# A decoder layer in three-pass fp32: the low halves of the weights made by accumulating DMAs instead of GpSimd

## The reference, cut to what matters

```python
x = x + 0.5 * swiglu(rms_norm(x, g_ffn1), w1_ffn1, w3_ffn1, w2_ffn1)     # 1024 -> 2816 -> 1024
z = rms_norm(x, g_mix) @ w_in + b_in                                     # 1024 -> 1792: q, k, v, u, v_gate
# head group A: windowed attention with sinks; head group B: gated spatial mixing in chunks of 128
x = x + concat(A, B) @ w_out + b_out
x = x + 0.5 * swiglu(rms_norm(x, g_ffn2), w1_ffn2, w3_ffn2, w2_ffn2)
x = x + sigmoid(rms_norm(x, g_ple) @ w_ple_gate) * (p @ w_ple_proj)
y = rms_norm(x, g_final)
```

## Time and profile before

| | |
|---|---|
| median of 3 runs | 1050.07 us (1049.6 to 1050.35) |
| span of the profiled execution | 1047.1 us, the one time that the page gives of it |
| PE busy | 1023.1 us, 98% |
| POOL busy | 473.8 us, 45% |
| DVE busy | 467.2 us, 45% |
| ACT busy | 340.0 us, 32% |
| DMA | 94.98 MB, 91 GB/s on average |
| chain that ended last | PE 93%, DVE 4%, ACT 1%, issue 1%, DMA 1% |

### The profile page before, as it was taken

One profiled execution on the slowest core, in us unless ns is written; L12 is line 12 of the kernel. 1 busy time (PEld: TensorE's weight loads), 2 busy tenths in 40 slices (PEclk: granted clock), 3 DMA queues, 4 the chain that ended last, 5 costly groups with the idle time before them and its releaser, 6 DMA issues.

```text
span 1047.1 us, 20237 instructions
## 1 busy us (share of the span) xinstructions
PE 1023.1 (98%) x8397; PEld 1009.3 (96%) x8397; DVE 467.2 (45%) x631; ACT 340.0 (32%) x505; POOL 473.8 (45%) x221
## 2 busy tenths in 40 slices
PE   6999999999999999999999999999999999999996
PEld 5999999999999999999989999999999999999895
DVE  6644544454421212356776554444454421121675
ACT  5222232223222222564534232223222322222232
POOL 2443434444455554321438444444444455555451
PEclk9999999999999999999999999999999999999998
DMA  5333232323232236322123232323233233323202
GB/s 177 100 89 97 83 100 80 100 80 121 71 96 90 90 95 181 88 60 61 41 72 101 81 102 81 100 82 98 85 95 91 86 91 96 90 90 96 85 22 82
DMA packets 179861, 94.98 MB, mean 91 GB/s; under 512 B 12010, under 2 KB 177220, under 8 KB 179804
## 3 DMA queue, kind: packets, MB, share of 16 engines
q1 hardware_dynamic: 175792, 90.76, 29.6%
q10 hardware_dynamic: 4028, 3.63, 1.1%
HBM read 91.82 MB, written 3.59 MB: 91 GB/s over the span
## 4 chain that ended last, share of the span: by engine, by line
PE 93%; DVE 4%; ACT 1%; issue 1%; DMA 1%; SPq 0%; DVEq 0%; ACTq 0%
PE ps L1126 89%; PE ps L1163 1%; PE ps L1364 1%; DMA x_rows<-in_x_prompt_dram 1%; PE ps L1337 1%; DVE rs_t L777 0%; PE ps L1158 0%; DVE mix_lo L1015 0%; DVE rs_i L774 0%; PE ps L1152 0%; DVE xg_lo L811 0%; DVE p_lo L1080 0%; DVE g_rows L985 0%; ACT xg_hi L491 0%; PE ps L1385 0%
## 5 line engine op out<-in xcount | busy, mean ns | idle before, releaser
L677 POOL TENSOR_TENSOR w_lo<-w_raw,w_hi 128x1024 fp32r<-128x1024 f32 x168 | 410.0, 2441 | 525.4 <-ACT w_hi L421 525.4
L1126 PE MATMUL ps<-xg_hi,w_hi 128*128 128x260 f32 x1760 | 360.3, 286 | 0.0
L1126 PE MATMUL ps<-xg_hi,w_lo 128*128 128x260 f32 x1760 | 355.9, 284 | 0.0
L1126 PE MATMUL ps<-xg_lo,w_hi 128*128 128x260 f32 x1760 | 355.3, 284 | 0.0
L421 ACT ACTIVATE w_hi<-w_raw 128x1024 fp32r<-128x1024 f32 x168 | 178.0, 1059 | 422.5 <-PE ps L1126 422.4
L1126 PEld LDWEIGHTS ps<-xg_hi,w_hi 128*128 128x128 f32 x1760 | 272.5, 190 | 1.3 <-issue 0.8
L1126 PEld LDWEIGHTS ps<-xg_hi,w_lo 128*128 128x128 f32 x1760 | 272.8, 189 | 0.0
L1126 PEld LDWEIGHTS ps<-xg_lo,w_hi 128*128 128x128 f32 x1760 | 271.8, 189 | 0.0
L1126 PE MATMUL ps<-h_hi,w_hi 128*128 128x260 f32 x704 | 142.0, 283 | 0.0
L1126 PE MATMUL ps<-h_hi,w_lo 128*128 128x260 f32 x704 | 141.5, 282 | 0.0
L1126 PE MATMUL ps<-h_lo,w_hi 128*128 128x260 f32 x704 | 141.3, 282 | 0.0
(11 more groups left out here) (209 smaller groups left out, 684.7 us busy)
## 6 DMA issues: line engine op xcount, KB each, us to landing
w_raw<-in_w_ffn_dram SPq DMA_DIRECT2D x120, 512.0 KB, 3.8
w_raw<-in_w_ffn_dram SPq DMA_DIRECT2D x16, 384.0 KB, 3.1
w_raw<-in_w_in_dram SPq DMA_DIRECT2D x10, 512.0 KB, 3.8
w_raw<-in_w_ple_gate_dram SPq DMA_DIRECT2D x8, 512.0 KB, 3.6
x_rows<-in_x_prompt_dram SPq DMA_DIRECT2D x4, 512.0 KB, 5.2
w_raw<-in_w_in_dram SPq DMA_DIRECT2D x8, 256.0 KB, 3.6
w_raw<-in_w_out_dram SPq DMA_DIRECT2D x16, 128.0 KB, 2.9
w_raw<-in_w_out_dram SPq DMA_DIRECT2D x8, 256.0 KB, 3.1
```

Source lines behind the costliest of these rows:

```text
L677: nc.gpsimd.tensor_tensor(w_lo[:, n % RING, :], w_raw[:, n % RING, :], w_hi[:, n % RING, :].bitcast(F32), ALU.subtract).then_inc(w_lo_read ...
L1126: ins = pe.matmul(ps[:, 2 * p + h, 0:HALF], w[:, n % RING, k * P:(k + 1) * P], m_[:, sk, h * HALF:(h + 1) * HALF], start=(first and i == 0 ...
```

## The change

ACT writes the negated high half into `w_lo` beside the high half into `w_hi`. POOL no longer subtracts: it starts a DMA that adds `w_raw` onto `w_lo`, so that `w_lo` holds raw - high. Its completion counts 16 on one of three semaphores `lo_in`, one for each slot; SP's loads and PE's units wait for those in place of `w_lo_ready`. `w_hi_ready` now counts when both ACT instructions are done. POOL's loops over the FFN units are written out. Nothing else differs.

```diff
-        w_hi_ready, w_lo_ready = sem("w_hi_ready"), sem("w_lo_ready")
+        w_hi_ready = sem("w_hi_ready")
+        lo_in = [sem(f"lo_in{i}") for i in range(RING)]
...
             def load(n, step, it, src, width=KD * P):
 
                 if n >= RING:
-                    sp_.wait_ge(w_lo_ready, at(n - RING + 1, step, it))
+                    sp_.wait_ge(lo_in[n % RING], at(16 * (n // RING), 16 * step // RING, it))
...
                     act.wait_ge(unit_done, at(n - RING + 1, step, it))
-                nc.scalar.activation(w_hi[:, n % RING, :], w_raw[:, n % RING, :], ACT.Copy).then_inc(w_hi_ready, 1)
+                nc.scalar.activation(w_hi[:, n % RING, :], w_raw[:, n % RING, :], ACT.Copy)
+                nc.scalar.activation(w_lo[:, n % RING, :], w_raw[:, n % RING, :], ACT.Copy,
+                                     scale=-1.0).then_inc(w_hi_ready, 1)
...
                 pool.wait_ge(w_hi_ready, at(n + 1, step, it))
-                nc.gpsimd.tensor_tensor(w_lo[:, n % RING, :], w_raw[:, n % RING, :],
-                                        w_hi[:, n % RING, :].bitcast(F32), ALU.subtract).then_inc(w_lo_ready, 1)
+                pool.dma_start(w_lo[:, n % RING, :], w_raw[:, n % RING, :],
+                               accum_op=ALU.add).then_inc(lo_in[n % RING], 16)
...
             def ffn(up, down, stat):
-                split_lo(up + 3)
-                split_lo(up + 4)
-                with pool.Fori(0, (KF - 1) // 3) as it:
-                    for r in range(3):
-                        split_lo(up + 2 * (1 + r) + 3, 6, it)
-                        split_lo(up + 2 * (1 + r) + 4, 6, it)
+                for n in range(up + 3, up + 2 * KF + 3):
+                    split_lo(n)
                 clear_ssq(stat + 1)
-                with pool.Fori(0, KD // 2) as it:
-                    for m in range(2):
-                        for c in range(3):
-                            split_lo(down + 3 * m + 3 + c, 6, it)
-                        add_square(stat + 1, m, 2, it)
+                for m in range(KD):
+                    for c in range(3):
+                        split_lo(down + 3 * m + 3 + c)
+                    add_square(stat + 1, m)
...
-                pe.wait_ge(w_lo_ready, at(n + 1, step, it))
+                pe.wait_ge(lo_in[n % RING], at(16 * (n // RING + 1), 16 * step // RING, it))
```

More of the change, by code:

```diff
@@ L360, in _ @@
                     n, j = IN + u, int(name[1])
-                    sp_.wait_ge(w_lo_ready, n - RING + 1)
+                    sp_.wait_ge(lo_in[n % RING], 16 * (n // RING))
                     for c in range(NKV):
@@ L1252, in _ @@
                             pe.wait_ge(z_scaled, u - 1 if u > 3 else 1)
-                        pe.wait_ge(w_lo_ready, n + 1)
+                        pe.wait_ge(lo_in[n % RING], 16 * (n // RING + 1))
                     if u == 0:
```

## The result

The changed kernel takes 1053.75 us, the median of 11 runs (1052.92 to 1060.40); the kernel before, run beside it, takes 1049.77 (11 runs, 1047.70 to 1051.29). The medians lie 4.0 us apart. The ratio is 1.0057, with a 95% interval of 1.0038 to 1.0075: slower, by 4 to 8 us. The ratio weighs all runs, here and in the experiments, and is larger than that of the medians because five of the 11 runs lie above 1055. The profiled execution took 1053.27 us and spans 1051.5. The result lies inside the predicted range, but on the other side of no change from the forecast of 1048.0.

The account below looks back on a forecast made before the run. PE was taken to bound the kernel, busy 1023.1 of 1047.1 us. Span 1047.1 - 4.8 (gains) + 2.7 (losses) = 1045.0, plus 3.0 from span to median run, gave 1048.0 us; range 1044.5 to 1085.

Parts of the forecast that it names:

- IN+3, and all FFN units, fit: Low halves, 7.5 us from high-half start, arrive within the room (8.1 us at mixer unit IN+3): no loss.
- T: Time from POOL's issue of the accumulating DMA to its completion, taken as 5.4 us.
- unit 0: First weight unit: low half ready at 20.9 in place of 19.44, a loss of 1.5 us.
- bound by engine time: Load 1.8 us plus accumulation at most twice that: 5.4 of a unit's 5.77 us on the DMA engines, close to full.
- Unit 2: Early weight unit with two more ACT copies ahead of it: a loss of 0.2 us.
- OUT+3: Output projection unit: low half needs 7.5 us of 6.5 us room, a loss of 1.0 us.
- Mixer: Gains at the spatial step: 1.3 us of PE's wait and 1.2 us from the lower clock behind it.
- stat_out and p: PE's waits for the diagonal ahead of stat_out, 1.6 us, and for p's low half, 0.7 us, go.
- Ring too short: Rival, chance 0.29: the weight ring is too short for the DMA, slower; it decides from T = 6.4.
- Gains do not come: Rival, chance 0.13: POOL still holds VectorE or mixer waits only move; gains of 4.8 shrink to 2, 1050.5 to 1052 us.
- VectorE holds up the issue: Rival, chance 0.06: POOL waits for VectorE instructions when issuing, T grows by 2.1 to 7.5, 1053.5 us.
- The DMA is quick: Rival, chance 0.12: T at most 4.4, hardly any loss, 1045.3 to 1046 us.

Follow-up runs that it names:

- Copies_late: Changed kernel with the two cache copies taken from ACT's burst at the mixer's start and issued by SP about 80 us later: 1050.89 us, ratio 1.0019.
- pool_in3: Changed kernel with the low half of unit IN+3 alone made by GpSimd's subtraction, without ACT's negated copy for it: 1049.28 us, ratio 1.0004.
- plain_copy: Changed kernel with GpSimd's 168 DMAs copying w_raw into w_lo, the addition left out: 1048.97 us in one execution.
- pool_three_late: Changed kernel with low halves of units 0, IN+3 and OUT+3 subtracted by GpSimd, cache copies issued 80 us later by SP: 1050.11 us, ratio 0.9996.
- pool_three_defer: pool_three_late with ACT's negated copy of unit IN+13 also moved behind the turned probabilities of the last attention item: 1046.99 us, ratio 0.9977.
- act_copy_only: Kernel before with ACT's negated copy into w_lo added and GpSimd adding w_raw instead of subtracting, no DMA: 1053.30 us, ratio 1.0044.

## Why the prediction failed where it did

**The step that failed** is "IN+3, and all FFN units, fit", as far as it speaks of IN+3. It was costed at 0, and the place cost 8.9 us, more than the whole distance from the forecast to the result (1053.75 - 1048.0 = 5.75). Copies_late and pool_in3 show that it is this place: the one takes its wait from 5.62 to 2.29 us, the other takes it away, and with it 6.9 of the 8.9 us and the measured loss. The other 2.0 come with a wait for ACT, which the prediction had at nothing as well. The step had three holes. It took T as one number for all places, from a median; the same engines carry the cache copies there, and T was 9.4. It took the start of the high half from before (417.73), although ACT issues DMAs ahead of it and one of those issues grew from 1.46 to 4.53 us. And it priced the clock only as a gain. The range held because it reached to a T of 9.3; but the forecast behind that upper end, all units paying, is not what happened. That the result lies in it is luck.

**T itself** was well sized: 5.4 forecast, 5.7 measured, unit 0 at 4.7. From the start of a high half to POOL's issue it is 2.3 us (420.93 to 423.22), 2.1 forecast. The bound by engine time also held: 48.1 + 30.2% of the engines, and no FFN unit waits. The second operand was costed at 1.8 us on a base of 3.8; plain_copy shows 2.8 on a base of 2.9, so two errors cancelled, and the median was met by luck. On the rule quoted there (the Trainium skill, DMA: Bandwidth & Descriptors, the anatomy of one DMA): the estimate of 3.2 us from it is near the 2.9 of the plain copy, and does not hold for the accumulating one.

**Losses.** Unit 0: 1.5 forecast, a wait of 1.23 and +0.5 against before. Unit 2: 0.2 forecast, no wait. OUT+3: 1.0 forecast, a wait of 0.50 and 0.8 in the table. FFN units: none, as forecast.

**Gains.** They came. Mixer: 1.3 + 1.2 forecast, 3.7 in the table. The stretch at the lower clock behind the spatial wait (532.2 to 535.6 in the kernel before) is gone; the window of the earlier trace rows has after

```profile
532.00:536.00 4.00, 4.00 (x33) 3.86 (x34) 3.37 (x5) 1.87 (x4) 2.00 (x3) 1.00 0.41 76
```

33 matmuls for 23. Last stage, stat_out and p: 1.6 + 0.7 forecast, 2.4 measured. The wait for probabilities grew from 0.5 to 1.4, forecast 1.5. What the prediction did not see in it is that it can bring the lower clock with it, for 10.2 us, in some executions: about 5 us then. By their profiles this is why pool_in3 and pool_three_late, which are rid of the wait at IN+3, reach the 1049 to 1050 of the kernel before and not the forecast of 1048.0; pool_three_defer, with that wait at 0.4 us, reaches 1046.99.

**Balance.** Losses 0.5 + 8.9 + 0.8, gains 3.7 + 2.4: 4.1 of the 4.4 us between the two spans.

**Rivals.** *Ring too short*: its sign came true, its mechanism at one crowded place only, with T at its median below the point from which it should decide (6.4). *Gains do not come*: not in the profile of after, where they came in full; but ACT's copies in the mixer's dense part, the reason given for it, did cost time. *VectorE holds up the issue*: no. An issue took 592 to 1010 ns (median 862) at every unit, in the FFNs while VectorE was at work:

```profile
L680 POOL DMA_DIRECT2D w_lo<-w_raw x168: 592/862/1010, 15.5 to 1019.3; - x168
```

The longest is 0.15 us above the median, so nothing kept an issue waiting by the 2.1 us that this rival needs, and T came out at 5.7 and not at its 7.5. The page's rule (the Trainium skill, SBUF — State Buffer, SBUF: two separate sides) ties that stall to VectorE operations in a mode that takes both ports; no row here tells which of this kernel's instructions run in such a mode. *The DMA is quick*: no.

**Open.** Of the 9.4 us at IN+3 some 2.6 are the cache copies (6.8 without them); what holds the rest above the median of 5.7 was not separated. Nor was it shown why bs_all's issue takes 4.5 us here. The new queue is not the whole of it: act_copy_only, which has no such queue, has 2.77 us for it, plain_copy 2.42, and the other kernels with accumulations 3.3 to 4.7. Why a wait of 1.4 us brings the lower clock in some executions of one kernel and not in others stays open too. That the long runs of after are such executions is argued from their mean granted clocks, 0.988 and 0.989 for the five above 1055 us against 0.991 to 0.995 for the others; none of them was profiled.

## What to carry to other kernels

A transfer that replaces an engine's instruction has no single duration: look, for each place where its room is small, at what else the DMA engines carry then and at what the issuing queues do ahead of it, and price a crowded place with little room by the slowest row, not by the median. Moving work to DMA can be done unit by unit: three tight units of 168 kept on GpSimd, two unrelated transfers moved and one copy put behind a critical ACT step turned a loss of 0.57% into a gain of 0.23%. In a kernel that keeps TensorE busy all the time, a new wait is to be priced with the clock that may fall behind it: a wait of 1.4 us cost here itself alone in some executions, and some 5 us more in others.

## What the runs showed of the hardware

- An accumulating DMA inside SBUF of 128 rows x 4 KB: 5.7 us to landing and 48.1% of the engines, against 2.9 us and 23.7% for the plain copy; GpSimd's issue 0.86 against 0.53 us. The Trainium skill (Collectives: The Full Stack, part on the bandwidth ceiling) says of reductions that they read two sources and so run at half the rate; the shares here, 2.03 to 1, agree.
- The FFNs' full weight loads on SP's queue landed in 5.2 us (median) beside it, and in 3.8 before and beside the plain copy.
- A DRAM-to-DRAM copy on another queue in packets of 65 KB, eight at a time for 2.4 to 3.7 us each, went with an accumulation of 9.4 us where it took 6.8 without; half of the accumulation's rows started only when the large packets ended.
- Between the start and the last microseconds, the stretches at the lower clock lasted 3.4, 6.8 or 10.2 us: 6.8 behind a wait of 5.4 or 5.6 us, 3.4 behind one of 2.3 (before and copies_late) and one of 1.7 (pool_three_late; none in pool_three_defer, with the same wait), and 10.2 behind the wait of 1.4 us in four profiles. After and act_copy_only had that wait of 1.4 us and no such stretch behind it. So the length of a wait alone does not tell whether the clock falls.
